# One seam wait, five reordered steps: how a two-block transformer kernel orders VectorE, ScalarE and TensorE around its first mixer

## The reference

```python
def first_block(x, ...):
    for l in range(DEPTH):                       # DEPTH = 2
        x = x + hybrid_mixer(rmsnorm(x, norm_mix[l]), w_in[l], ...)
        x = x + hierarchical_moe(rmsnorm(x, norm_ffn[l]), ...)
    return rmsnorm(x, norm_final)

def hybrid_mixer(h, w_in, sink, conv_w, g_attn, g_conv, w_out, cos, sin):
    q, k, v, gate_b, gate_c, u = jnp.split(h @ w_in, SPLITS, axis=-1)
    y_attn = windowed_gqa_with_sink(rope(q), rope(k), v, sink)        # 8 heads of 64
    y_conv = gate_b * centred_short_conv(gate_c * u, conv_w)
    return jnp.concatenate([rmsnorm(y_attn), rmsnorm(y_conv)], -1) @ w_out

def hierarchical_moe(h, ...):                    # 32 experts, each 3 matrices of 2 MB, top 2
    ...
    return segment_sum((silu(xb @ w_gate[e]) * (xb @ w_up[e])) @ w_down[e] * gate)
```

## Time and profile before

| quantity | value |
|---|---|
| median of three runs | 1917.3 us (1915.96 to 1917.67) |
| profiled execution, its own time | 1915.96 us |
| its span (first to last instruction) | 1914.2 us |
| TensorE busy | 1854.3 us, 97% |
| VectorE busy | 833.7 us, 44% |
| ScalarE busy | 670.1 us, 35% |
| bytes moved | 557.58 MB, mean 291 GB/s |

### The profile page before, as it was taken

The page is one execution under the profiler, slowest core; times in us unless marked ns, Lnnn a source line. Parts: engine busy times, 40 slices in busy tenths (PEclk is TensorE's granted clock), DMA queues, the critical chain, the costliest instruction groups (busy, mean ns, idle before and its releaser), DMA issues.

```text
span 1914.2 us, 28319 instructions
## 1 busy us (share of the span) xinstructions
PE 1854.3 (97%) x11306; PEld 1257.3 (66%) x11306; DVE 833.7 (44%) x1889; ACT 670.1 (35%) x1287; POOL 268.8 (14%) x239
## 2 busy tenths in 40 slices
PE   9999999999999999999999999999999999999998
PEld 8774444444447874444434446888989978888997
DVE  5763121211215762112211114566665655667655
ACT  5632111111114631111111113457664544575544
POOL 1400000000000400000000003972000057800000
PEclk9999999999999999999999999999999999999999
DMA  8569999999996469999999996452524845433353
GB/s 297 225 237 416 428 427 427 429 428 428 429 424 226 189 274 399 412 427 427 428 428 429 429 427 241 143 207 89 173 92 154 280 171 176 174 136 104 118 170 134
DMA packets 121430, 557.58 MB, mean 291 GB/s; under 512 B 5008, under 2 KB 49584, under 8 KB 96240
## 3 DMA queue, kind: packets, MB, share of 16 engines
q1 hardware_dynamic: 119696, 551.51, 72.5%
q10 hardware_dynamic: 1440, 4.36, 0.6%
q0 software_dynamic: 192, 0.30, 0.1%
HBM read 555.11 MB, written 1.05 MB: 291 GB/s over the span
## 4 chain that ended last, share of the span: by engine, by line
PE 58%; DVE 4%; DMA 3%; ACT 3%; issue 2%; POOL 0%; SPq 0%; POOLq 0%; DVEq 0%; ACTq 0%
PE bank L2322 7%; PE bank L2353 5%; PE bank L2471 3%; PE bank L2473 3%; PE bank L2472 3%; DMA ring<-w_up_dram 3%; PE bank L2450 3%; PE bank L2451 3%; PE bank L2452 3%; PE bank L2324 3%; PE bank L2557 3%; PE bank L2045 2%; PE bank L2420 2%; PE bank L2054 2%; PE bank L2487 1%
## 5 line engine op out<-in xcount | busy, mean ns | idle before, releaser
L2322 PE MATMUL bank<-ring,work 128*64 128x512 f32 x544 | 242.6, 601 | 13.4 <-issue 13.4
L1663 DVE TENSOR_TENSOR work<-work,bank 64x512 f32<-64x512 f32 x64 | 43.9, 685 | 440.0 <-ACT work L1004 440.0
L2324 PE MATMUL bank<-ring,work 128*64 128x512 f32 x512 | 232.3, 609 | 0.0
L776 POOL TENSOR_TENSOR stat<-stat,power 128x1 f32<-128x1 f32 (+1 forms) x18 | 10.8, 600 | 1496.5 <-DVE stat L1235 959.9
L816 POOL TENSOR_TENSOR w_lo<-ring,w_hi 128x512 fp32r<-128x512 f32 (+1 forms) x160 | 208.1, 1317 | 53.6 <-ACT w_hi L1054 50.8
L1004 ACT ACTIVATE work<-bank 64x512 f32<-64x512 f32 x64 | 37.8, 591 | 466.5 <-PE bank L2324 466.5
L1054 ACT CAST w_hi<-ring 128x512 fp32r<-128x512 f32 (+1 forms) x208 | 123.3, 606 | 120.8 <-PE bank L2473 81.5
L2353 PE MATMUL bank<-ring,work 128*64 128x512 f32 x480 | 155.8, 595 | 1.8 <-ACT work L1009 0.4
L2322 PEld LDWEIGHTS bank<-ring,work 128*64 128x64 f32 x544 | 73.1, 138 | 125.5 <-issue 123.6
L1883 DVE TENSOR_TENSOR w_lo<-ring,w_hi 128x512 fp32r<-128x512 f32 (+1 forms) x176 | 116.3, 678 | 79.0 <-ACT w_hi L1159 78.7
L1679 DVE SCALAR_TENSOR_TENSOR act_hi<-bank,stat,act_hi 128x512 fp32r<-128x512 f32 x64 | 48.1, 751 | 211.1 <-ACT act_hi L1014 211.1
(11 more groups left out here) (354 smaller groups left out, 4489.4 us busy)
## 6 DMA issues: line engine op xcount, KB each, us to landing
ring<-w_in_dram SPq DMA_DIRECT2D x34, 2048.0 KB, 9.0
ring<-w_gate_dram SPq DMA_DIRECT2D x34, 2048.0 KB, 21.1
ring<-w_up_dram SPq DMA_DIRECT2D x32, 2048.0 KB, 26.6
ring<-w_down_dram SPq DMA_DIRECT2D x30, 2048.0 KB, 26.0
ring_tail<-w_down_dram SPq DMA_DIRECT2D x18, 2048.0 KB, 24.1
work<-w_gate_dram SPq DMA_DIRECT2D x16, 2048.0 KB, 21.8
work<-w_up_dram SPq DMA_DIRECT2D x16, 2048.0 KB, 26.2
ring_tail<-w_up_dram SPq DMA_DIRECT2D x16, 2048.0 KB, 27.2
```

The source lines that it names most:

```text
L2322: pe.matmul(m_bank(m)[gate, :], lhs, wg[:, k], start=(k == 0), stop=(k == KD - 1), skip_group_check=True)
L2324: mu = pe.matmul(m_bank(m)[up, :], lhs, wu[:, k], start=(k == 0), stop=(k == KD - 1), skip_group_check=True)
```

## The change

Six places change; the arithmetic is the same.

1. `turn_h`, for the stages of the first block, now makes TensorE wait, right after the transposes of a row tile, until both banks of that tile are emptied. The wait in `query_half` goes.
2. VectorE makes four small constants (the slot numbers and the `causal` mask) after both normalisations of the first layer, no longer ahead of them.
3. In the first layer, ScalarE and VectorE handle all four hT banks before the first weight chunk (before: two banks, one chunk, two banks, three chunks).
4. At the end of the first layer's experts, VectorE computes the rests of the next mixer's four chunks ahead of adding the result to `x` (before: two between the adding and the normalisation, two behind the normalisation).
5. `logits(1)` on VectorE moves behind the rests of gate chunks 5 and `gated_input(1)`.
6. Output tile 0 stands beside head 6, tile 1 beside head 7, and tiles 2 and 3 behind the heads (before: 0 and 1, 2, and 3). The list of bank uses follows, and with it ScalarE's rounding of the second group of output chunks, now behind its reading of head 7's transposes.

```diff
-               [("out1", 0), ("out1", 1)], [("out1", 2)]]
+               [("out1", 0)], [("out1", 1)]]
...
-        names += [("out1", layer, 3)]
+        names += [("out1", layer, i) for i in (2, 3)]
...
-                round_hT(0)
-                round_hT(1)
+                for j in range(4):
+                    round_hT(j)
                 if layer == 0:
-                    round_chunks(range(1))
-                round_hT(2)
-                round_hT(3)
-                if layer == 0:
-                    round_chunks(range(1, CHUNKS))
+                    round_chunks(range(CHUNKS))
...
                 for j in range(4):
-                    if layer == 0 and j == 2:
-                        rest_of_chunks(layer, range(1))
...
-                    rest_of_chunks(layer, range(1, CHUNKS))
+                    rest_of_chunks(layer, range(CHUNKS))
...
                 gated_input(0)
-                logits(1)
                 rest_of_chunks(layer, gate_chunks(5))
                 gated_input(1)
...
                     if hh + 1 < HEADS:
-                        if hh > 0:
-                            logits(hh + 1)
+                        logits(hh + 1)
                         weights(hh + 1)
...
+                if layer + 1 < DEPTH:
+                    rest_of_chunks(layer + 1, range(CHUNKS))
                 for hf in range(2):
                     dve.wait_ge(M["scattered"], hf + 1)
...
-                if layer + 1 < DEPTH:
-                    rest_of_chunks(layer + 1, range(2))
                 for t in range(NT):
                     normalise(2 * layer + 2, t, h if layer + 1 < DEPTH else x)
-                if layer + 1 < DEPTH:
-                    rest_of_chunks(layer + 1, range(2, CHUNKS))
...
                     done(mm, name)
+                if stage < SECOND:
+                    for j in (2 * t, 2 * t + 1):
+                        emptied(pe, ("hT", stage, j))
...
                     for t in range(NT):
-                        emptied(pe, ("hT", 2 * layer, 2 * t + half))
                         query_half(half, t)
...
-                mixer_out(3)
+                for i in (2, 3):
+                    mixer_out(i)
```

More of the change, by code:

```diff
@@ L1266, in last_hT @@
                                 ).then_inc(psum_read[TILE[name] % BANKS], 1)
[L1268 to L1272, removed]
             for t in range(NT):
@@ L1275, in _ @@
                 normalise(0, t)
+            dve.wait_ge(masks_ready, 1)
             def second_block_tables():
@@ L1985, in second @@
                 scale_rows(stage + 1, 1)
+            S(dve.tensor_scalar(slot_number, iota_f[:], 1.0, None, ALU.add))
+            S(dve.tensor_scalar(causal[:, 0:P], before[:], NEG, None, ALU.mult))
+            S(dve.memset(causal[:, P:2 * P], 0.0))
+            S(dve.tensor_scalar(causal[:, 2 * P:], before[:], NEG, None, ALU.mult))
             S.settle()
```

## The result

The changed kernel takes 1934.99 us (median of four runs, 1932.25 to 1938.01) against 1917.49 us (1915.96 to 1918.04): 17.5 us more, ratio 1.0092 with a 95% interval of 1.0080 to 1.0104. The forecast was 1934.5, a loss of 18, in a range of 1926 to 1942. The changed kernel was run more often than that: over all its 23 runs the median is 1935.19, from 1932.04 to 1938.37, and the longest is the execution that was profiled. Its trace stands 22.4 above that of before and shows the loss at its larger end.

What follows compares the result with a forecast made beforehand. TensorE, busy 97% of the span, was taken to bound the kernel, its delays passing on one for one. 4.4 + 4.8 + 2.2 + 3.6 + 3.0 = 18.0 on 1915.96 gave 1934.0, taken as 1934.5; range 1926 to 1942.

Steps and rivals of the forecast that it cites:

- One for one: Ahead of the experts: TensorE's delay there delays the weight stream, and the end, by the same amount.
- The rival in which the experts absorb it: Experts of each layer: the weight stream sets their end and starts no later; no change, about 1917; chance 0.05.
- The start, 4.4 without the clock: Start of layer 0: first query product at 18.4 against 14.03, +4.4 us (4 to 6.3).
- The constants: Start of layer 0: four small VectorE operations ahead of its first rests, taken as 0.7 us for all.
- The seam, 4.8 without the clock: Seam to layer 1: first product at 597.3 against 592.50, +4.8 us (0.7 to 5.5).
- The 0.5 us returned ahead of the mean: Seam: the pair of chunk rests no longer stands ahead of the mean, giving back 0.5 of 2.4 us.
- `logits(1)`, 1.1 per layer: Head 1, both layers: the division arrives about 1.1 us after TensorE wants it, 2 x 1.1 = +2.2 us.
- the bound of 0.6: Head 1: lower bound of TensorE's wait per layer, with the division done in 1.0 us.
- The tiles, 1.8 per layer: Head 7's transposes, both layers: TensorE stands 1.8 us for VectorE's division, 2 x 1.8 = +3.6 us.
- The clock, 3.0: Start and seam: pauses pull TensorE's granted clock down, +3.0 us, bounds 0 and 7.4.
- the upper bound of 7.4: Clock loss at start and seam: 1.7 us and another 2.0 for slow zeros and transposes, twice.
- The forecast of 1.5 per place: Clock loss taken at each of start and seam, 1.5 us; a fall among the experts cost 1.7.

Runs made afterwards that it cites:

- with the clock held: The changed kernel with TensorE multiplying zeros through the new pauses, the waits staying: 1931.39 us against 1916.83, ratio 1.0075.
- part 1 alone: The kernel before with only TensorE's wait behind each row tile's transposes until both banks are emptied: 1926.44 us against 1917.51, ratio 1.0046.
- part 4 alone: The kernel before with only the four chunk rests ahead of the additions: 1918.29 us against 1917.51, ratio 1.0002.
- part 5 alone: The kernel before with only logits(1) moved behind the chunk rests and gated_input(1): 1919.49 us against 1917.51, ratio 1.0012.
- part 6 alone: The kernel before with only output tiles 0 and 1 beside heads 6 and 7, 2 and 3 behind: 1920.77 us against 1917.51, ratio 1.0015.

## Why the prediction was right, step by step

- **One for one.** Right. The transfers were idle at 145 to 153 us as they were at 134 to 142, and the experts' end moved by 11.14 after 10.93 ahead of them. The rival in which the experts absorb it is out. From the sum of squares to the last scatter, router and experts of layer 0 took 480.42 us before and 480.63 now, and over the twelve profiled kernels 479.75 to 483.24 (layer 1: 480.09 to 483.19), whether TensorE came early or late. So a single trace tells the end of a layer to 3.5 us only; the 0.21 of the table is no measure of what is passed on, the unshrunk duration is.
- **The start, 4.4 without the clock.** Measured 4.06 with the clock held; the reference in before varies by 0.7 from execution to execution, so this agreement is partly luck. The constants took 0.5, not 0.7: VectorE's first rests began at 11.48 instead of 10.97.
- **The seam, 4.8 without the clock.** Measured 4.79 with the clock held. The 0.5 us returned ahead of the mean is in it: the transposes came 1.93 later after the last scatter (13.07 - 11.14), for 1.9 predicted.
- **`logits(1)`, 1.1 per layer.** Measured 1.07 and 1.08. The division was slower still beside POOL (1.14 for the pair), so the bound of 0.6 did not come. The operation of POOL that the prediction leans on in the earlier trace rows starts at 51.21, as the division ends; the one that ran beside it in the kernel before is this:

```profile
50.21 0.92 POOL L796 TENSOR_SCALAR work<-work,cols 128x256 f32<-128x256 f32 x1
```

- **The tiles, 1.8 per layer.** The stall is 1.85, and 1.88 and 1.85 alone; in the changed kernel the stage shows 1.63 and 1.66, since the wait at head 5 shrank by about a fifth of a microsecond. That small give-back was not in the working.
- **The clock, 3.0.** 2.9 in the medians. In the profiled execution it was 4.2 at the start and 3.6 at the seam: 7.8, above the upper bound of 7.4, and it brought the first query product to 21.02 where 18 to 19 was forecast (18.13 with the clock held). The forecast of 1.5 per place was taken from single falls among the experts, and that the medians lie so near it is in part luck. That it varies from run to run, and with it the time, I had not said. For part 1 alone I then expected too much of it.
- The sum of the parts alone is 8.9 + 0.8 + 2.0 + 3.3 + 0.5 = 15.5 of 17.5. The other 2 are about what the interval of a single one of these measurements allows (1.8 us and more to either side), and were not traced to one place. That the long pause ahead of the transposes (part 4) and those behind them (part 1) meet only in the whole kernel may be the cause; it was not tried.

## What to carry to other kernels

Ask of a wait not only how long it lasts but what is queued behind it on its engine: the filler work meant to cover a pause must stand ahead of the wait, and moving the wait alone was worth 5.9 us here. When a chain alternates between engines, don't take work put into a gap for free: look whether another engine's operation in flight beside it gets longer (POOL's root, 0.56 to 0.95), and whether something downstream needs the work that it pushes back (the convolution's rest, a wait of 0.6). And before a stall is called hidden behind a saturated transfer, look whether the transfer's first step waits for the stalled engine.

## What the runs showed of the hardware

- Whether the clock falls after a pause differs from one execution to the next. In the profiled executions it fell to 0.50 behind the seam's pause of 3.23 or 3.24 us in all four kernels that have it, though by the mean clocks not in most runs of part 4 alone; behind 6 of 8 pauses of 2.17 to 2.28 us among the experts, in the trace of before and in that of the changed kernel alike; and behind one of ten pauses of 1.84 or 1.85 us at head 7 (five kernels, two layers each). Filling the pauses with zero products kept it at 1.00 at the start and the seam.
- TensorE's first 22 zero products took 4.54 to 5.07 us in the profiled kernels, 0.21 to 0.23 each, with the granted clock shown as 1.00; the 32 at the seam took 3.73, 0.12 each. The position of head 0 doesn't follow them: with 5.07 it came at 46.19 (part 5 alone), with 4.86 at 46.88 (part 4 alone). In the two late ones of the five kernels with the start of before, ScalarE's rounding of the first chunk waited for its transfer, and the second chunk's product then for VectorE's rest (part 6 alone):

```profile
12.06 0.62 ACT L866 CAST w_hi<-ring 128x512 fp32r<-128x512 f32 x1 [0.75 <-DMA ring<-w_in_dram]
...
15.35 0.50 PE L2064 MATMUL bank<-w_hi,stream 128*128 128x512 f32 x1 [0.45 <-DVE w_lo L1332]
```

- POOL's inverse root on 128x1 took 0.56 us alone and 0.95 beside a VectorE subtraction with both inputs in fast memory. The Trainium skill, page "SBUF — State Buffer", section "Who interferes with whom", has this: a VectorE instruction with two inputs in SBUF contends with a GpSimd instruction that reads SBUF. The slower root agrees. So work that VectorE does in the gap of 0.7 us in which it waits for POOL is paid for in part by a longer root.
